# Six projections of two transformer blocks in units of 512 rows by 512 columns, with fox values behind the fox queries and keys

## The chip, the cores and the metric

The kernel runs on 1 core of a Trainium2 chip. The metric is the device time of one execution in microseconds (us). Three runs of the kernel before took 976.42, 976.95 and 977.11 us, median 976.95.

## The reference

The kernel computes two blocks in sequence on 256 tokens of width 1024, in float32. What matters here are the projections of the normed tokens and what uses them:

```python
h = _rmsnorm(x, norm_mix_g[l])
z = h @ w_in[l]                      # 1024 -> hq hf hi hg | fq fk fv ff | mq | gates
(hq, hf, hi, hg, fq, fk, fv, ff, mq, gate_logits) = jnp.split(z, pts, axis=-1)
y_a = _hgrn2_mixer(hq, hf, hi, hg, lower_bounds[l], hgrn_norm_g[l])      # 4 heads of 128
y_b = _fox_mixer(fq, fk, fv, ff, ...)     # 8 heads of 64, softmax of q.k + decay, causal
mem_kv = _rmsnorm(mem, norm_mem_g[l]) @ mem_kv_w[l]                      # mk, mv
y_c = _memory_mixer(mq, mem_kv, ...)      # 4 heads of 128, attention into 256 memory rows
merged = sum(gates[:, :, i] * (y_i @ w_br_i))
x = x + merged @ w_out;  x = x + conv_glu_ffn(rmsnorm(x))
# second block
x = x + 0.5 * swiglu(rmsnorm(x))
qa, ka, va, qb, kb, vb = split(rmsnorm(x) @ w_in_2)   # each 512 wide
x = x + concat(diff_attention(qa, ka, va), dilated_attention(qb, kb, vb)) @ w_out_2
x = rmsnorm(x + 0.5 * swiglu(rmsnorm(x)))
```

Each of hg, hi, fv, mq, mv and vb is one product of a 256 x 1024 matrix with a 1024 x 512 one, with tokens as rows of the result. fq and fk need a root mean square over each head before they meet.

## The kernel before, in words

**Split products.** Every product is done to float32 accuracy by splitting both operands into a high and a low part. `three` issues three matmuls for each 128 rows of the contraction: high by high, high by low, low by high.

**Units.** The weights are a list of units of 128 x 2048 elements (1 MB), made by `weight_plan`. SyncE's queue loads a unit into `raw`, of which there are three; ScalarE writes its high part into `wh` (L975, called by `begin` and `hi_to`), VectorE the low part into `wl` (L1415, `lo_to`). TensorE waits for `w_lo` before it uses a unit, and ScalarE writes unit j when TensorE has ended unit j - 3 (`unit_end`). `begin(key)` on ScalarE and VectorE stands for: prepare the units up to two behind `key`. Since each engine works through its instructions in order, the place of a `begin` is also the place at which everything behind it may wait.

**A projection.** A projection of 512 columns is two units of all 1024 rows by 256 columns. `toks_out` (tokens as rows of the result) takes one bank of the PSUM, and for each half m of the tokens it issues 8 x 3 matmuls of 256 columns, with the transposed normed tokens `hT` as stationary side. ScalarE empties the bank with two instructions (`toks_scaled`, L1009 and L1010), each scaled by the token's norm. `W` (banks 0 and 1) and `WF` (0, 1, 6, 7) hand out banks in turn. `mid` is a function that `toks_out` calls between the two halves; it puts small attention matmuls between the large ones.

**The fox stage** (fox and memory attention of the first block, 141 to 250 us). TensorE issues fq 0, fk 0, fv 0, two transposes for the hgrn branch (`turn(("rd", p))`), fq 1, the transposes of the normed heads (`head_turn`), fk 1 and so on. ScalarE's `head_norm` empties a bank and squares it (L1140), VectorE's `head_sum` adds the squares up (L1720), and GpSimd makes the inverse root (`head_rstd`, L2151 to L2162) and scales the heads (`head_scaled`, L2212). ScalarE also writes the forget sums into the keys for all heads (`fk_made`, two instructions at L1168), VectorE those of the queries (`fox_row`, eight at L1739), and copies the transposed heads out of the PSUM (`fox_out`, L1734). Only then can `scores(0, 0)` run (L656). Behind it come the minimum of the scores (`guards`, L1785), the exponentials (`exps`, L1154), the division (`shares`, L1750), the transposes (`turns`, L670), their `copies` (L1797) and the products with the values (`pair_values`, L703). `step(a, s, t, vs)` issues on TensorE the scores of map s, the values of the maps vs and the transposes of map t.

**The end of the second mixer** (735 to 770 us). vb 0 and vb 1 alternate with the last steps; then come the output projection's units `wo`, which already have 512 rows by 512 columns: `stretch` issues 12 matmuls of 512 columns for one half of the tokens (`weight_wide`), and `half_done` counts the units that end in the middle of a sum.

Of the kernel before, what the change touches and what calls it, by code (L numbers as in the profile page):

```python
# [92 lines left out]

def weight_plan(I):
    w_in, w_in2 = I["w_in"], I["w_in_2"]
    plan = []
    plan += [(("hf", u), cols(w_in, 512 + 256 * u)) for u in range(2)]
    plan += [(("hq", u), cols(w_in, 256 * u)) for u in range(2)]
    plan += [(("hg", u), cols(w_in, 1536 + 256 * u)) for u in range(2)]
    plan += [("ff", cols(w_in, 3584, 8))]  # L100
    plan += [(("hi", u), cols(w_in, 1024 + 256 * u)) for u in range(2)]
    plan += [(("gate", u), cols(w_in, 4104 + 256 * u)) for u in range(12)]
    for u in range(2):
        plan += [((name, u), cols(w_in, a + 256 * u)) for name, a in (("fq", 2048), ("fk", 2560), ("fv", 3072))]
    plan += [(("mq", u), cols(w_in, 3592 + 256 * u)) for u in range(2)]
# [4 lines left out]
    plan += [(("mv", u), cols(I["mem_kv_w"], 512 + 256 * u)) for u in range(2)]  # L110
# [4 lines left out]
    for name, u, a in (("qa", 0, 0), ("ka", 0, 512), ("va", 0, 1024), ("qa", 1, 0), ("ka", 1, 512), ("va", 1, 1024),  # L115
                       ("qb", 0, 1536), ("kb", 0, 2048), ("qb", 1, 1536), ("kb", 1, 2048), ("vb", 0, 2560), ("vb", 1, 2560)):
        plan += [((name, u), cols(w_in2, a + 256 * u))]
    plan += wide_units(4, I["w_out_2"])
# [12 lines left out]
def build(nc, plan, I, out):  # L131
    ctx = ExitStack()
    with ctx:
# [218 lines left out]
        def pe_program(pe):  # L352
# [88 lines left out]

            def turn(key, src, p, n, split=True):
# [90 lines left out]
            for u in range(2):  # L533
                toks_out(("hg", u), WF)
# [9 lines left out]
            toks_out(("hi", 0), WF)  # L544
# [6 lines left out]
            toks_out(("hi", 1), WF)  # L551
# [157 lines left out]
            def mem_values(i):  # L709
                h = i - 8  # L710
                if h % 2 == 0:
                    take(("mo", h // 2), 6 + h // 2, False)
                    turn_no["mo", h // 2] = len(turn_no) + 1
                    pe.wait_ge(*free(("mv", h // 2)))
# [39 lines left out]
            for key in (("fq", 0), ("fk", 0), ("fv", 0)):  # L754
                toks_out(key, W)
# [16 lines left out]
            toks_out(("mq", 0), W, mid=other_fox_heads)  # L772
            step(0, 4, 3)
            toks_out(("mq", 1), W, mid=lambda: step(0, 5, None, [2, 3]))
# [162 lines left out]
            toks_out(("vb", 0), W, mid=lambda: step(1, 12, 10))  # L937
# [4 lines left out]
            toks_out(("vb", 1), W, mid=lambda: step(1, 14, 12, [8, 9]))  # L942
            step(1, 15, 13, [10, 11])
# [7 lines left out]
            step(1, None, 14)  # L951
# [11 lines left out]
        def act_program(act):  # L963
# [47 lines left out]

            def gained_hi(p, g, made):
# [43 lines left out]
            for u in range(2):  # L1056
                begin(("hg", u))
                s = v3(Sg[:, :])[:, :, u * 256:u * 256 + 256]
                if u == 0:
                    act.wait_ge(rstd_made, 1)  # L1060
                toks_scaled(s, ("hg", u), rs0)
                act.wait_ge(*seq.now())
                act.wait_ge(*free(("hg", u)))
                act.activation(v3(P[u][:, :]), s, ACT.Sigmoid).then_inc(g_sig, 1)
# [8 lines left out]
            toks_scaled(v3(Iv[:, :])[:, :, 0:256], ("hi", 0), rs0)  # L1073
# [8 lines left out]
            toks_scaled(v3(Iv[:, :])[:, :, 256:512], ("hi", 1), rs0)  # L1082
# [48 lines left out]

            def head_norm(name, u, src, dst, sq):
                n = HEADS.index((name, u))
# [4 lines left out]
                if n >= 2:  # L1138
                    act.wait_ge(h_sum, n if n >= 6 else n - 1)
                act.activation(v3(sq), d, ACT.Square).then_inc(h_sq, 1)  # L1140
# [21 lines left out]
            begin(("fv", 0))  # L1162
            toks_scaled(v3(Vt[:, :])[:, :, 0:256], ("fv", 0), rs0)

            act.wait_ge(*free("fcum"))
            for j in range(2):
                r = ROW[1 - j]
                act.activation(Kf[j].rearrange("p (k n) -> p k n", k=4)[r], F2[r, :].unsqueeze(1).to_broadcast([64, 4, 256]),  # L1168
                               ACT.Identity, scale=fsel[r, 16:17], bias=fsel[r, 17:18]).then_inc(fk_made, 1)
            for p in range(2):  # L1170
                turn_hi_part(("rd", p), yTh, p, col("hg"))
# [1197 lines left out]
```

## Time and profile before

| | |
|---|---|
| runs of the kernel before | 976.42, 976.95, 977.11 us |
| the profiled execution | 976.5 us, its span 974.7 us |
| TensorE busy | 959.8 us (98%), 6422 matmuls |
| TensorE's weight loads | 858.2 us (88%) |
| VectorE busy | 710.2 us (73%) |
| ScalarE busy | 519.4 us (53%) |
| GpSimd busy | 68.7 us (7%) |
| the chain that ended last | TensorE 94%, VectorE 3%, ScalarE 2% |
| DMA | 174.17 MB, mean 179 GB/s |

Matmuls are pipelined, so one is still shown as running when the next has begun: a single 256-column matmul is shown with 0.28 us but the next begins 0.12 us later. TensorE's pace is read from the distance of the starts.

### The profile page before, as it was taken

The page shows a single profiled execution, that of the slowest core. Times are in us where ns is not written, and L with a number is a line of the kernel's source. Part 1 is how long each engine was busy: PE and PEld are TensorE (multiplying, and loading weights), DVE is VectorE, ACT ScalarE, POOL GpSimd, SP SyncE. Part 2 cuts the span into 40 slices and gives each one's busy share as a digit, 9 for nine tenths or more (in the row PEclk, how much of TensorE's full clock was granted, in tenths as well). Part 3 has the DMA queues.
Part 4 walks back from the last instruction along what each step waited for, and adds up shares of the span by engine and source line. Part 5 has one row for each costly group of instructions (what it writes and reads, how often), then busy time and mean ns, then how long its engine had stood idle before and what let it go on. Part 6 is the DMA issues. An engine that isn't in the chain of part 4 may idle for free.

```text
span 974.7 us, 15574 instructions
## 1 busy us (share of the span) xinstructions
PE 959.8 (98%) x6422; PEld 858.2 (88%) x6422; DVE 710.2 (73%) x1013; ACT 519.4 (53%) x658; POOL 68.7 (7%) x150
## 2 busy tenths in 40 slices
PE   7999999999999999999999999999999999999997
PEld 7999999999988888888888888889999788888886
DVE  5589767886777877787786667567678678576666
ACT  6565757555446656554664444446545554443544
POOL 0010223233210000000000000000002000000000
PEclk9999999999999999999999999999999999999999
DMA  9754444443465564655456555553433546555541
GB/s 345 260 177 151 173 155 149 163 144 127 173 227 173 210 216 173 210 179 186 160 175 214 176 206 180 183 198 134 177 131 130 182 143 216 198 190 178 191 151 44
DMA packets 26534, 174.17 MB, mean 179 GB/s; under 512 B 3552, under 2 KB 3808, under 8 KB 6368
## 3 DMA queue, kind: packets, MB, share of 16 engines
q1 hardware_dynamic: 25744, 170.14, 50.0%
q10 hardware_dynamic: 720, 3.04, 0.8%
q8 instruction: 51, 0.84, 0.3%
q14 instruction: 19, 0.16, 0.0%
HBM read 172.12 MB, written 1.05 MB: 178 GB/s over the span
## 4 chain that ended last, share of the span: by engine, by line
PE 94%; DVE 3%; ACT 2%; issue 0%; DMA 0%; POOL 0%; ACTq 0%; DVEq 0%; POOLq 0%
PE ps L371 50%; PE ps L381 25%; PE ps L382 13%; PE ps L656 2%; DVE wl L1415 1%; PE ps L449 1%; PE ps L670 1%; ACT wh L975 1%; PE ps L703 1%; PE ps L573 1%; DMA GT<-in_gains 0%; PE ps L717 0%; PE ps L684 0%; DVE HG L1645 0%; PE ps L463 0%
## 5 line engine op out<-in xcount | busy, mean ns | idle before, releaser
L1415 DVE TENSOR_TENSOR wl<-raw,wh 128x2048 fp32r<-128x2048 f32 x153 | 348.2, 2277 | 66.5 <-ACT wh L975 65.9
L381 PE MATMUL ps<-hT,wh 128*128 128x512 f32 x1056 | 371.5, 395 | 0.2 <-DVE hT L1444 0.2
L975 ACT ACTIVATE wh<-raw 128x2048 fp32r<-128x2048 f32 x156 | 296.3, 1900 | 76.0 <-PE ps L371 70.8
L382 PE MATMUL ps<-hT,wl 128*128 128x256 f32 x1056 | 295.8, 280 | 0.0
L381 PEld LDWEIGHTS ps<-hT,wh 128*128 128x128 f32 x1056 | 198.0, 188 | 46.8 <-issue 0.6
L382 PEld LDWEIGHTS ps<-hT,wl 128*128 128x128 f32 x1056 | 199.4, 189 | 1.2
L371 PE MATMUL ps<-hT,wh 128*128 128x256 f32 (+1 forms) x912 | 170.6, 289 | 7.0 <-DVE wl L1538 6.6
L371 PEld LDWEIGHTS ps<-hT,wh 128*128 128x128 f32 (+1 forms) x912 | 142.7, 192 | 8.7 <-DVE wl L1538 6.6
L371 PE MATMUL ps<-wh,hT 128*128 128x256 f32 (+1 forms) x704 | 142.3, 296 | 1.3 <-DVE wl L1415 1.3
L371 PE MATMUL ps<-hT,wl 128*128 128x256 f32 (+1 forms) x456 | 129.6, 284 | 0.0
L1261 ACT ACTIVATE Am<-ps 128x512 f32<-128x512 f32 x66 | 39.1, 593 | 151.7 <-PE ps L382 149.0
L371 PE MATMUL ps<-wl,yTh 128*128 128x512 f32 (+1 forms) x298 | 117.7, 395 | 0.0
L371 PEld LDWEIGHTS ps<-wh,hT 128*128 128x128 f32 x704 | 113.4, 191 | 4.6 <-issue 2.0
L371 PE MATMUL ps<-wh,yTl 128*128 128x512 f32 (+1 forms) x298 | 117.2, 393 | 0.0
L371 PE MATMUL ps<-wh,yTh 128*128 128x512 f32 (+1 forms) x298 | 117.0, 393 | 0.0
L371 PE MATMUL ps<-wl,hT 128*128 128x256 f32 (+1 forms) x352 | 102.9, 292 | 0.0
L1500 DVE TENSOR_TENSOR PT<-ps,Am 128x256 f32<-128x256 f32 x132 | 49.8, 419 | 69.5 <-ACT Am L1261 69.3
L371 PEld LDWEIGHTS ps<-hT,wl 128*128 128x128 f32 (+1 forms) x456 | 87.3, 192 | 0.2
L371 PEld LDWEIGHTS ps<-wl,hT 128*128 128x128 f32 x352 | 67.3, 191 | 1.2
L371 PEld LDWEIGHTS ps<-wh,yTh 128*128 128x128 f32 x298 | 55.9, 188 | 13.5
L371 PEld LDWEIGHTS ps<-wh,yTl 128*128 128x128 f32 x298 | 55.9, 188 | 12.9
L371 PEld LDWEIGHTS ps<-wl,yTh 128*128 128x128 f32 x298 | 56.0, 188 | 12.0
(253 smaller groups left out, 819.7 us busy)
## 6 DMA issues: line engine op xcount, KB each, us to landing
raw<-in_units SPq DMA_DIRECT2D x155, 1024.0 KB, 4.8
BIGT<-in_bias ACTq DMA_DIRECT2D x1, 2048.0 KB, 7.5
XT<-in_x_turned SPq DMA_DIRECT2D x4, 256.0 KB, 4.7
raw<-in_units SPq DMA_DIRECT2D x4, 256.0 KB, 5.3
raw<-in_units SPq DMA_DIRECT2D x2, 512.0 KB, 7.6
X<-in_x SPq DMA_DIRECT2D x1, 1024.0 KB, 8.2
Hn<-in_mem SPq DMA_DIRECT2D x1, 1024.0 KB, 11.0
XT<-in_mem_turned SPq DMA_DIRECT2D x1, 1024.0 KB, 12.9
```

What stands on the lines that cost most here:

```text
L371: ins = pe.matmul(o, l(k), r(k), start=first and k == ks[0] and j == 0, stop=last and k == ks[-1] and j == 2)
L381: pe.matmul(o, lh(k), hT_both(k), start=first and k == ks[0], stop=False)
L382: ins = pe.matmul(o[:, 256:512], ll(k), hT_at(k)[0], start=False, stop=last and k == ks[-1])
L449: ins = pe.transpose(t[:, q * 128:q * 128 + 128], src[:, m * n + k * 128:m * n + k * 128 + 128], ident)
L573: ins = pe.matmul(t[x:x + w, q * w + w - z:q * w + w], s[:, x:x + w], s[:, x + a:x + a + z], start=True, stop=True)
L656: ins = pe.matmul(t[:, x:z], l, r, start=True, stop=True)
L670: ins = pe.transpose(t[:, j * 128:j * 128 + 128], src[:, o:o + 128], ident)
L703: ins = pe.matmul(o[64 * j:64 * j + 64, 128 * kb:256], v[:, x:x + 64], turned(a, i + j)[:, c], start=kb == 0, stop=kb == 1)
L975: act.activation(wh[j % NS][:, 0:n], raw[j % NR][:, 0:n], ACT.Copy).then_inc(w_hi, 1)
L1261: act.activation(v3(crossed_out(n)), t, ACT.Copy).then_inc(cross_made, 1)
L1415: dve.tensor_tensor(wl[j % NS][:, 0:n], raw[j % NR][:, 0:n], wh[j % NS][:, 0:n].bitcast(F32), ALU.subtract).then_inc(w_lo, 1)
L1500: dve.tensor_tensor(d[:, m, :], t[:, m, :], v3(crossed_out(n))[:, m, :], ALU.add).then_inc(*emptied((key, key + ("x",))[m]))
```

## The change

Six projections (hg, hi, fv, mq, mv, vb) get units of 512 rows by 512 columns. The first unit holds rows 0 to 511 of all columns, the second the rest. `toks_wide` replaces `toks_out` for them: it takes two banks, one for each half m of the tokens, and a unit issues 2 x 4 x 3 matmuls of 512 columns. The sums of both halves stay open between the two units, so both banks are emptied in or after the second unit; the first unit ends with `half_done`. ScalarE empties a bank of 128 x 512 with one instruction (`wide_scaled`).

```diff
+def wide_rows(name, w, a):
+    return [((name, r), block(w, 512 * r, 512, a, 512)) for r in (0, 1)]
...
+            def toks_wide(name, r, banks, mid=None):
+                i = U[name, r]
+                if r == 0:
+                    bs = [banks.take(), banks.take()]
+                weights(i)
+                for m in range(2):
+                    t = take((name, m), bs[m]) if r == 0 else bank[at[name, m][0]]
+                    ins = three(t[:, :], left(hT_at, m), weight_wide(i, r), EIGHT[4 * r:4 * r + 4], r == 0, r == 1)
+                    if r:
+                        ins.then_inc(ps_full[at[name, m][0]], 1)
+                    if m == 0 and mid:
+                        mid()
...
+            def wide_scaled(dst, name, rs, ms=(0, 1)):
+                for m in ms:
+                    act.wait_ge(*full((name, m)))
+                    act.activation(dst[:, m * 512:m * 512 + 512], bank[at[name, m][0]][:, :], ACT.Copy,
+                                   scale=rs[:, m:m + 1]).then_inc(*emptied((name, m)))
```

The fox stage is written in another order on TensorE:

```diff
-            for key in (("fq", 0), ("fk", 0), ("fv", 0)):
+            for key in (("fq", 0), ("fk", 0), ("fq", 1)):
                 toks_out(key, W)
             pe.wait_ge(ya_made, 2)
             for p in range(2):
                 turn(("rd", p), Sg, p, 512)
-            toks_out(("fq", 1), W)
+            toks_out(("fk", 1), W)
             head_turn("fq", 0, E0)
             head_turn("fk", 0, E1)
-            toks_out(("fk", 1), W, mid=lambda: step(0, 0))
+            toks_wide("fv", 0, W, mid=lambda: step(0, 0))
             step(0, 1)
-            toks_out(("fv", 1), W, mid=lambda: step(0, 2, 0))
+            toks_wide("fv", 1, W, mid=lambda: step(0, 2, 0))
```

and at the end of the second mixer the values of maps 8 to 11 move behind the first output stretch, since they now need vb whole:

```diff
-            toks_out(("vb", 1), W, mid=lambda: step(1, 14, 12, [8, 9]))
-            step(1, 15, 13, [10, 11])
+            toks_wide("vb", 1, W, mid=lambda: step(1, 14, 12))
+            step(1, 15, 13)
...
-            step(1, None, 14)
+            step(1, None, 14, [8, 9, 10, 11])
```

ScalarE and VectorE follow. In both, mq's two squares and the two sums now come together, after mq's second unit. On ScalarE, this is the fox stage before, from the square of fk 0 (L1140 Am) to the high part behind the transposes (HG and Vm at L1168 are the broadcasts of the forget sums; wh is the high part of a weight unit):

```order
L1140 ACTIVATE Am<-HG 128x512 [waits ps_free1,a_seq]
L975 ACTIVATE wh1<-raw1 128x2048 [waits raw_in1,ps_full1]
L1009 ACTIVATE Vt<-ps,sm 128x256 [waits ps_full0]
L1010 ACTIVATE Vt<-ps,sm 128x256
L1168 ACTIVATE HG<-F2,C 64x1024 [waits ps_free2]
L1168 ACTIVATE Vm<-F2,C 64x1024
L982 ACTIVATE yTh<-ps,VT 128x512 [waits ps_full3]
L982 ACTIVATE yTh<-ps,VT 128x512 [waits ps_full4]
L975 ACTIVATE wh2<-raw2 128x2048 [waits raw_in2,ps_full0]
L1009 ACTIVATE HG<-ps,sm 128x256 [waits ps_full1]
```

and now (the lines are 26 to 33 higher):

```order
L1166 ACTIVATE Am<-HG 128x512 [waits ps_free1,a_seq]
L1199 ACTIVATE HG<-F2,C 64x1024 [waits ps_free2]
L1199 ACTIVATE Vm<-F2,C 64x1024
L1001 ACTIVATE wh1<-raw1 128x2048 [waits raw_in1,ps_full1]
L1035 ACTIVATE HG<-ps,sm 128x256 [waits ps_full0]
L1036 ACTIVATE HG<-ps,sm 128x256
L1166 ACTIVATE Ax<-HG 128x512 [waits h_sum,ps_free0,a_seq]
L1008 ACTIVATE yTh<-ps,VT 128x512 [waits ps_full3]
L1008 ACTIVATE yTh<-ps,VT 128x512 [waits ps_full4]
L1001 ACTIVATE wh2<-raw2 128x2048 [waits raw_in2,ps_full0]
L1035 ACTIVATE HG<-ps,sm 128x256 [waits ps_full1]
```

The broadcasts now follow the square of fk 0 directly. They stand ahead of the high part of the stage's fifth unit (fk 1 before, fv 0 now), and the eviction into Vt is gone from here.

On VectorE, the same stage before, from the last of the eight fox rows (L1739) to the first guard (L1436 makes the low parts of rd, L1720 is a head sum, L1734 are the copies of the transposed heads, wl is the low part of a weight unit):

```order
L1739 TENSOR_SCALAR Iv<-F2,C 64x256
L1436 SCALAR_TENSOR_TENSOR yTl<-ps,VT,yTh 128x512 [waits turn_hi] x2
L1734 TENSOR_SCALAR HG<-ps,VT 64x512 [waits ps_full5]
L1734 TENSOR_SCALAR Iv<-ps,VT 64x512
L1734 TENSOR_SCALAR HG<-ps,VT 64x512 [waits ps_full2]
L1734 TENSOR_SCALAR Vm<-ps,VT 64x512
L1415 TENSOR_TENSOR wl2<-raw2,wh2 128x2048 [waits w_hi]
L1785 ISA ps,sm<-ps,C 128x128 [waits ps_full3]
```

and now:

```order
L1776 TENSOR_SCALAR Iv<-F2,C 64x256
L1757 TENSOR_REDUCE sm<-Ax 128x8 [waits h_sq]
L1473 SCALAR_TENSOR_TENSOR yTl<-ps,VT,yTh 128x512 [waits turn_hi] x2
L1452 TENSOR_TENSOR wl2<-raw2,wh2 128x2048 [waits w_hi]
L1757 TENSOR_REDUCE sm<-Am 128x8 [waits h_sq]
L1771 TENSOR_SCALAR HG<-ps,VT 64x512 [waits ps_full5]
L1771 TENSOR_SCALAR Iv<-ps,VT 64x512
L1771 TENSOR_SCALAR HG<-ps,VT 64x512 [waits ps_full2]
L1771 TENSOR_SCALAR Vm<-ps,VT 64x512
L1452 TENSOR_TENSOR wl0<-raw0,wh0 128x2048 [waits w_hi]
L1822 ISA ps,sm<-ps,C 128x128 [waits ps_full3]
```

Two sums and one low part of a weight unit stand between the last fox row and the copies into HG, Iv, HG and Vm; the low part that stood behind the copies is still there.

On TensorE, the end of vb before (L703 is the product with the values, L670 the transposes, L371 with yTh the first output stretch):

```order
L656 MATMUL ps<-HG 128x128 [waits ps_free5]
L656 MATMUL ps<-HG 128x256
L703 MATMUL ps<-Hn,Vm 64x256 [waits ps_free4,ps_free2]
L703 MATMUL ps<-Hn,Vm 64x256
L703 MATMUL ps<-Hn,Vm 64x128 x2
L670 MATMUL ps<-C,P1 128x128 [waits share_made,ps_free2]
L670 MATMUL ps<-C,P1 128x128 x2
L371 MATMUL ps<-wh1,yTh 128x512 [waits ps_free5,w_lo,ps_free2,ps_free1,ps_free0]
```

and now, up to the output stretch:

```order
L682 MATMUL ps<-HG 128x128 [waits ps_free5]
L682 MATMUL ps<-HG 128x256
L696 MATMUL ps<-C,P1 128x128 [waits share_made,ps_free2]
L696 MATMUL ps<-C,P1 128x128 x2
L377 MATMUL ps<-wh1,yTh 128x512 [waits ps_free5,w_lo,ps_free2,ps_free1,ps_free0]
```

The values between the scores and the transposes are gone, and the output stretch waits for the same banks.

## Rows read from the trace of the kernel before

**Rows 1.** The page, part 1: busy us (share of the span) and instructions.
```profile
PE 959.8 (98%) x6422; PEld 858.2 (88%) x6422; DVE 710.2 (73%) x1013; ACT 519.4 (53%) x658; POOL 68.7 (7%) x150
```

**Rows 2.** Timeline of TensorE: start, us, engine, line, op, out<-in, count, idle before.
```profile
33.60 0.36 PE L371 MATMUL ps<-wh,hT 128*128 128x256 f32 x1 [1.32 <-DVE wl L1415]
...
45.18 0.40 PE L371 MATMUL ps<-hT,wh 128*8 128x256 f32 x2
...
275.21 0.40 PE L371 MATMUL ps<-wh,hT 128*128 128x512 f32 x1
...
280.70 0.39 PE L371 MATMUL ps<-wh,yTh 128*128 128x512 f32 x1
```

**Rows 3.** The chain that ended last, at the first gates: start, us, what.
```profile
64.41 2.19 DVE wl L1415
66.74 5.99 PE ps L371 x48
```

**Rows 4.** Timeline of ScalarE in the fox stage.
```profile
153.97 1.90 ACT L975 ACTIVATE wh<-raw 128x2048 fp32r<-128x2048 f32 x1
...
159.13 1.24 ACT L1168 ACTIVATE HG<-F,C 64x1024 f32<-64x1024 f32 x1
...
161.54 1.24 ACT L982 ACTIVATE yTh<-ps,VT 128x512 fp32r<-128x512 f32 x2
```

**Rows 5.** Timeline of VectorE in the fox stage.
```profile
158.22 0.42 DVE L1739 TENSOR_SCALAR HG<-F,C 64x256 f32<-64x256 f32 x1
...
161.34 0.40 DVE L1739 TENSOR_SCALAR Iv<-F,C 64x256 f32<-64x256 f32 x1
162.24 1.41 DVE L1436 SCALAR_TENSOR_TENSOR yTl<-ps,VT,yTh 128x512 fp32r<-128x512 f32 x2 [0.50 <-ACT yTh L982]
165.34 0.74 DVE L1734 TENSOR_SCALAR HG<-ps,VT 64x512 f32<-64x512 f32 x1 [1.69 <-PE ps L449]
...
168.47 2.29 DVE L1415 TENSOR_TENSOR wl<-raw,wh 128x2048 fp32r<-128x2048 f32 x1
...
171.38 0.68 DVE L1720 TENSOR_REDUCE sm<-Ax 128x8 f32<-128x512 f32 x1
```

**Rows 6.** Timeline of GpSimd in the fox stage; of GpSimd and VectorE at 744.
```profile
162.18 2.06 POOL L2212 TENSOR_TENSOR HG<-HG,sm 128x512 f32<-128x512 f32 x2
...
743.92 1.90 POOL L2244 TENSOR_TENSOR Sg<-Sg,sm 128x1024 f32<-128x1024 f32 x1
...
744.03 2.14 DVE L1750 TENSOR_SCALAR P<-P,sm 128x128 f32<-128x128 f32 x2
```

**Rows 7.** The chain that ended last, at the first fox scores.
```profile
168.65 0.89 PE ps L656 x4
```

**Rows 8.** Timeline of VectorE and ScalarE at maps 1 to 3.
```profile
174.18 0.29 DVE L1785 CUSTOM_DVE_ANT_0 ps<-ps,C 128x128 f32<-128x128 f32 x1
...
175.75 1.92 ACT L975 ACTIVATE wh<-raw 128x2048 fp32r<-128x2048 f32 x1
...
180.54 0.30 DVE L1785 CUSTOM_DVE_ANT_0 ps<-ps,C 128x128 f32<-128x128 f32 x1
...
181.80 0.55 DVE L1750 TENSOR_SCALAR P<-P,sm 128x128 f32<-128x128 f32 x2
```

**Rows 9.** Timeline of all engines at the end of vb.
```profile
751.23 0.87 PE L703 MATMUL ps<-Hn,Vm 128*64 128x256 f32 x8
...
755.03 0.55 DVE L1750 TENSOR_SCALAR P<-P,sm 128x128 f32<-128x128 f32 x2
...
755.86 0.47 ACT L1010 ACTIVATE Vm<-ps,sm 128x256 f32<-128x256 f32 x1
...
757.14 0.48 PE L371 MATMUL ps<-wh,yTh 128*128 128x512 f32 x1
...
760.02 0.82 PE L670 MATMUL ps<-C,P 128*128 128x128 f32 x6
```

**Rows 10.** TensorE in a window: us, busy (instructions), granted clock, DMA, GB/s.
```profile
6.60:11.00 4.40, 4.36 (x20) 1.00 1.02 359
```

More of the change, by code:

```diff
@@ L109, in weight_plan @@
     plan += [(("mk", u), cols(I["mem_kv_w"], 256 * u)) for u in range(2)]
-    plan += [(("mv", u), cols(I["mem_kv_w"], 512 + 256 * u)) for u in range(2)]
+    plan += wide_rows("mv", I["mem_kv_w"], 512)
     plan += branches[0][1:] + branches[1] + branches[2]
@@ L936, in pe_program @@
             step(1, 11, 9)
-            toks_out(("vb", 0), W, mid=lambda: step(1, 12, 10))
+            toks_wide("vb", 0, W, mid=lambda: step(1, 12, 10))
             step(1, 13, 11)
@@ L1057, in act_program @@
                 begin(("hg", u))
-                s = v3(Sg[:, :])[:, :, u * 256:u * 256 + 256]
+                s = Sg[:, u * 512:u * 512 + 512]
                 if u == 0:
                     act.wait_ge(rstd_made, 1)
-                toks_scaled(s, ("hg", u), rs0)
-                act.wait_ge(*seq.now())
+                wide_scaled(Sg, "hg", rs0, (u,))
                 act.wait_ge(*free(("hg", u)))
-                act.activation(v3(P[u][:, :]), s, ACT.Sigmoid).then_inc(g_sig, 1)
+                act.activation(P[u][:, :], s, ACT.Sigmoid).then_inc(g_sig, 1)
             begin("ff")
@@ L1129, in act_program, with head_squares @@
                 gate_sigmoid(j)
+            def head_squares(name, u, d, sq):
+                n = HEADS.index((name, u))
+                if n >= 2:
+                    act.wait_ge(h_sum, n if n >= 6 else n - 1)
+                act.activation(v3(sq), d, ACT.Square).then_inc(h_sq, 1)
             def head_norm(name, u, src, dst, sq):
-                n = HEADS.index((name, u))
                 d = v3(dst)[:, :, u * 256:u * 256 + 256]
@@ L1169, in act_program @@
                                ACT.Identity, scale=fsel[r, 16:17], bias=fsel[r, 17:18]).then_inc(fk_made, 1)
+            begin(("fq", 1))
+            head_norm("fq", 1, rs0, E0, sq_a)
             for p in range(2):
                 turn_hi_part(("rd", p), yTh, p, col("hg"))
-            begin(("fq", 1))
-            head_norm("fq", 1, rs0, E0, sq_a)
             begin(("fk", 1))
+            head_norm("fk", 1, rs0, E1, sq_b)
+            begin(("fv", 0))
             exps(0, 0)
-            head_norm("fk", 1, rs0, E1, sq_b)
             exps(0, 1)
             begin(("fv", 1))
+            wide_scaled(Vt, "fv", rs0, (0,))
             exps(0, 2)
-            toks_scaled(v3(Vt[:, :])[:, :, 256:512], ("fv", 1), rs0)
+            wide_scaled(Vt, "fv", rs0, (1,))
             exps(0, 3)
             begin(("mq", 0))
-            act.wait_ge(*full(("ht", "fq", 0)))
-            head_norm("mq", 0, rs0, E0, sq_a)
             exps(0, 4)
             begin(("mq", 1))
+            for u in range(2):
+                act.wait_ge(*full(("ht", "fq", u)))
+            wide_scaled(E0, "mq", rs0, (0,))
             exps(0, 5)
-            act.wait_ge(*full(("ht", "fq", 1)))
-            head_norm("mq", 1, rs0, E0, sq_b)
+            wide_scaled(E0, "mq", rs0, (1,))
+            for m in range(2):
+                act.wait_ge(*free(("mq", m)))
+            for u, sq in enumerate((sq_a, sq_b)):
+                head_squares("mq", u, v3(E0)[:, :, u * 256:u * 256 + 256], sq)
             exps(0, 6)
@@ L1832, in dve_program @@
             shares(0, 1)
-            begin(("fv", 1))
             guards(0, 3)
```

69 lines of the change are left out of this document (36 added, 33 removed).

## The prediction

> **What bounds the kernel.** I read the page first. TensorE is busy 98% of the span [rows 1], so the question is which of its instructions get cheaper and where it will have to wait. The second view is TensorE's timeline, for its pace, since the durations of overlapping matmuls overstate it. From the first narrow matmul of hg to the first of ff, the 96 matmuls of 256 columns take 45.18 - 33.60 = 11.58 us, 0.121 us each. In the output projection, 24 matmuls of 512 columns with hT as the stationary side take 280.70 - 275.21 = 5.49 us, 0.229 us each [rows 2]. So a matmul costs about 13 ns beyond its columns, and half as many matmuls save that. The third view is the chain of waits and the timelines of VectorE and ScalarE, for how far the cover reaches where instructions change places: in the fox stage TensorE and VectorE already meet within 0.2 us.
>
> **Part 1, the wide units.** A projection was two units of 48 narrow matmuls and becomes two units of 24 wide ones: 11.58 - 2 x 5.49 = 0.6 us less each, 3.6 us for six [rows 2]. The bound below this is a pace as with yT as stationary side, about 0.1 us less per unit, so 1.3 us less in all. The weight units keep their number and size; each still costs ScalarE 1.90 us and VectorE 2.29 us [rows 4, 5] in units of 5.5 us, hidden behind matmuls. The evictions are as many columns in half as many instructions, also hidden.
>
> The Trainium skill ("TensorE: Matmul & The Clock Gate", section "Back-to-back issue gap") gives a spacing of N/2.4 + 2.5 ns. By that fixed part the 288 matmuls saved would be worth 0.7 us and not 3.6; rows 2 show about 13 ns, and I go by them.
>
> **Part 2, hg and hi.** TensorE gets through them 1.2 us earlier, but after that the first gates wait for VectorE: the low part of gate unit 1 is made after the scan, ends at 66.60, and TensorE begins at 66.74 [rows 3]. This chain starts at hg's last eviction, about 0.6 us earlier now, and ScalarE leaves hi's first eviction out of it. I move it by 0.7 us, and TensorE gains only this: **-0.7 us** (bounds 0 and -1.2).
>
> **Part 3, the fox stage, which decides.** Three moves act together. ScalarE's two broadcasts into the keys (L1168) now stand ahead of the high part of the stage's fifth unit (now fv's first), where they stood behind it. VectorE's low part of that unit stands ahead of the eight fox rows, as before, so these now wait for the broadcasts too. And ahead of the four copies that the first scores need (fox_out), VectorE now has two head sums (fq 1 and fk 1) and one more low part. Step by step, on the clock of the profile before:
> - ScalarE starts the broadcasts at 153.97, where it started the high part; they take 161.54 - 159.13 = 2.4 us, then the high part 1.90: ready at 158.3 [rows 4].
> - VectorE: low part 2.3, to 160.6. Eight fox rows: 161.34 + 0.40 - 158.22 = 3.5 [rows 5]. They now fall under GpSimd's two products, 2.06 us [rows 6]. At 744.03 a tensor_scalar that reads SBUF took 2.14 us beside a GpSimd product that began at 743.92 [rows 6], and 0.55 otherwise [rows 8]. Fully blocked adds 2.1, not at all 0; I take 1.4, since it is blocked in that row but the eight rows would be somewhat faster without GpSimd's small instructions. To 165.5.
> - Sum of fq 1 0.6, low parts of rd 1.35, low part of a unit 2.25, sum of fk 1 0.6, and four copies 168.47 - 165.34 = 3.1 [rows 5]: to 173.4. Scores begin 0.2 later, at 173.6.
> - TensorE is there at 168.5, since the wide half unit ends as the narrow one did; before, its scores began at 168.65 [rows 7]. **Wait: 5.1 us** (bounds 3.6 and 5.8).
>
> Behind this wait stand the other half of fv's first unit and all that follows on TensorE; nothing later on the path has slack to give it back, as TensorE is the bound everywhere.
>
> A second wait follows at the transposes of head 1. From the start of scores 1 TensorE has about 7.8 us of its own work to them. The other side has the scores (0.7), guard and exponential 1.6 (174.18 to 175.75), the high part 1.90 and low part 2.29 of mq's second unit, which now stand ahead of guard 2, and then guard, copy and share, 1.8 (180.54 to 182.35) [rows 4, 5, 8]: 8.3, with the latencies 8.5. **Wait: 0.7 us** (bounds 0 and 1.3).
>
> mq's two squares and sums now come together after its last matmul. That puts the scaled heads 0.6 us later relative to TensorE, but TensorE has two branch stretches and mk's first unit before it turns them, more than 10 us: no cost. fv and mq save 4 units x 0.3. Sum of the stage: 5.1 + 0.7 - 1.2 = **+4.6 us** (bounds 2.4 and 5.9).
>
> **Part 4, mv.** Each half is used late, and nothing near it waits: **-0.6 us**.
>
> **Part 5, vb.** The values of maps 8 to 11 need vb whole and move behind the first output stretch. VectorE's share of map 13 ends at about 755.5, and it does not come earlier, since its chain runs over VectorE and ScalarE. TensorE, without 2 x 0.8 us of values [rows 9], arrives at 754.9 and waits; turns, then the output stretch from 756.2, when ScalarE has emptied vb's second bank (755.5 plus 0.6; before, 755.86 + 0.47, and the stretch at 757.14), 2.8 us, then 1.6 us of values: 760.6 at the transposes that began at 760.02 [rows 9]. **+0.6 us** in spite of wide units (bounds -0.6 and +0.9).
>
> **Sum.** -0.7 + 4.6 - 0.6 + 0.6 = +3.9 us. The profiled execution took 976.5 us (span 974.7), so 980.4; it is 0.45 below the median of the runs, 976.95, so a median of 980.9. About 0.2%, 2 us, is the least that a measurement of this kernel tells from no change.
>
> **Rivals.**
> - *The clock falls in the wait.* In its first 4.4 us TensorE ran 20 matmuls [rows 10], one per 0.213 us, against 0.120 later: the lower level (1.2 GHz) after 6.6 us of nothing, though the granted clock in the row says 1.00. A wait of 1.3 us at 33.60 [rows 2] did not bring this back. 5.1 us lies between. If it does, 20 x 0.093 = 1.9 us more: 982.8. For it: by far the longest wait in the program. Against it: no wait in this trace shows it. The Trainium skill has it as a rule (same page, "Part 1: The HAM clock gate"): idle time throttles the array again.
> - *The queue is in time, and the change is not slower.* If the fox rows run before the broadcasts' high part is waited for, or ScalarE gets the broadcasts in earlier, both fox waits vanish and only the sums of saved overhead are left: -0.7 - 1.2 - 0.6 + 0.6 = -1.9, so 975.0. The point that decides is the end of the fox copies on VectorE: if it comes before 169.4, when the wait is under 1.2 us and the total under zero. Against it: VectorE is an in-order queue, and the 15 us of work between 158.3 and the copies' end are counted from rows.
> - *The wait is there but shorter.* GpSimd does not block the fox rows and the second wait falls away: 980.9 - 1.4 - 0.7 = 978.8.
> - *The wide matmul is no faster here.* 512 columns at yT's pace: 980.9 + 1.3 = 982.2.
>
> **Chances.** Forecast 0.45; clock 0.17; shorter wait 0.14; no wait 0.14; pace 0.10. The predicted time is the forecast's, 980.9. Its own range is 979.6 to 982. The range takes in the clock's case and the shorter wait's: 977.8 to 983.3. Faster by over 0.2% 0.13 (the case without waits, some of it within), within 0.2% 0.12, slower 0.75.
>
> **What would show it.** In the profile after: TensorE's timeline has an idle stretch of about 5 us before the first fox scores, ended by VectorE's last fox copy; the broadcasts stand right behind fk 0's square on ScalarE; fox rows spaced wider beside GpSimd's products; 24 wide matmuls of a hT unit take 5.5 us; gate unit 1 begins about 0.7 us earlier; the second output projection begins its first stretch earlier and its last transposes later. If the idle before the scores is under 1.2 us, the prediction is wrong in Part 3; if matmuls behind it are spaced as in the first 4 us, the clock rival is right.

## The result and the profile after

| | before | after |
|---|---|---|
| median of four runs each | 976.94 us (976.42 to 977.11) | 984.30 us (983.75 to 984.40) |
| the profiled execution, its span | 976.5, 974.7 us | 984.21, 982.4 us |
| mean granted clock over the span | 0.999 | 0.995 |

The ratio is 1.0077, with a 95% interval of 1.0065 to 1.0089: slower by 7.4 us, where 3.9 were forecast. The direction and the place were right and the size was not.

Part 1 of the page after, to be held against [rows 1]. TensorE has 288 matmuls fewer, and the sum of their durations is not less:

```profile
PE 960.3 (98%) x6134; PEld 844.4 (86%) x6134; DVE 711.1 (72%) x1013; ACT 517.0 (53%) x646; POOL 68.7 (7%) x150
```

The view of TensorE's waits (engine, line, what it waited for: us in total, times, longest) has three larger kinds that the kernel before did not have, those for "issue", for VectorE's P and for GpSimd's HG (two more, for VectorE's Vm and HG, are of 0.2 us each and are left out here):

```profile
PE ps L682 <- issue: 4.9, 1, 4.9
...
PE ps L696 <- DVE P L1787: 1.4, 2, 0.9
PE ps L475 <- POOL HG L2249: 0.3, 1, 0.3
```

"issue" is the name of the largest of the three. It means only that the view found no releaser. VectorE's timeline names it. The last of the four fox copies (L1771) ends at 171.99 + 0.76 = 172.75, and the scores (L682) begin at 172.96. These rows of VectorE after (start, duration, then as in the rows before) answer to [rows 5]:

```profile
157.96 2.29 DVE L1452 TENSOR_TENSOR wl<-raw,wh 128x2048 fp32r<-128x2048 f32 x1 [3.65 <-ACT wh L1001]
160.28 0.42 DVE L1776 TENSOR_SCALAR HG<-F,C 64x256 f32<-64x256 f32 x1
...
161.17 1.02 DVE L1776 TENSOR_SCALAR HG<-F,C 64x256 f32<-64x256 f32 x1
162.23 1.02 DVE L1776 TENSOR_SCALAR Iv<-F,C 64x256 f32<-64x256 f32 x1
...
164.62 0.41 DVE L1776 TENSOR_SCALAR Iv<-F,C 64x256 f32<-64x256 f32 x1
164.95 0.67 DVE L1757 TENSOR_REDUCE sm<-Ax 128x8 f32<-128x512 f32 x1
165.54 1.39 DVE L1473 SCALAR_TENSOR_TENSOR yTl<-ps,VT,yTh 128x512 fp32r<-128x512 f32 x2
166.86 2.27 DVE L1452 TENSOR_TENSOR wl<-raw,wh 128x2048 fp32r<-128x2048 f32 x1
169.06 0.67 DVE L1757 TENSOR_REDUCE sm<-Am 128x8 f32<-128x512 f32 x1
169.66 0.73 DVE L1771 TENSOR_SCALAR HG<-ps,VT 64x512 f32<-64x512 f32 x1
...
171.99 0.76 DVE L1771 TENSOR_SCALAR Vm<-ps,VT 64x512 f32<-64x512 f32 x1
```

It is the queue of the prediction, item by item. VectorE waits 3.65 us for the high part, which stands behind the broadcasts. Then come the low part, eight fox rows, a sum, the low parts of rd, another low part, a sum, and only then the copies. Two of the eight fox rows take 1.02 us instead of 0.42, beside GpSimd's products.

On TensorE, what follows that wait is as important as the wait:

```profile
167.63 0.39 PE L377 MATMUL ps<-wh,hT 128*128 128x512 f32 x1
172.96 1.62 PE L682 MATMUL ps<-HG 128*128 128x128 f32 x4 [4.93 <-issue]
174.02 0.99 PE L377 MATMUL ps<-wh,hT 128*128 128x512 f32 x1
174.80 0.63 PE L377 MATMUL ps<-wl,hT 128*128 128x512 f32 x1
175.23 1.05 PE L377 MATMUL ps<-wh,hT 128*128 128x512 f32 x2
176.08 0.63 PE L377 MATMUL ps<-wl,hT 128*128 128x512 f32 x1
...
178.92 0.81 PE L682 MATMUL ps<-Vm,Iv 128*128 128x128 f32 x4
```

From 174.80 to 176.08 three wide matmuls begin, (176.08 - 174.80) / 3 = 0.427 us each; in the unit of [rows 2] it was 0.229. The windows of the same trace (stretch, length, busy time of each engine, granted clock, DMA share, GB/s) show the clock ahead of the wait, behind it and one stretch later:

```profile
165.00:167.90 2.90, 2.90 (x15) 2.17 (x13) 2.90 (x5) 2.80 (x4) 0.00 (x0) 1.00 0.00 0
174.80:178.00 3.20, 3.20 (x9) 2.52 (x8) 1.07 (x5) 0.91 (x4) 2.88 (x5) 0.50 0.59 159
179.40:182.30 2.90, 2.90 (x14) 2.40 (x13) 1.31 (x7) 1.75 (x5) 0.00 (x0) 1.00 0.00 0
```

0.50 of 2.4 GHz is the lower level, 1.2 GHz. The Trainium skill ("TensorE: Matmul & The Clock Gate", section "Back-to-back issue gap") gives a spacing of N/1.2 ns for that level; by it 512 columns are an estimated 427 ns, and the trace agrees, with 427.

Where the 7.7 us between the two spans came in is read from the starts of the same instruction on TensorE in both timelines (us):

| instruction | before | after | difference | what came in since the row above |
|---|---|---|---|---|
| first level products of the hgrn branch (L573, now L599) | 72.66 | 72.16 | -0.50 | hg and hi |
| fox scores of map 0 | 168.65 | 172.96 | +4.31 | the first wait |
| fox scores of map 1 | 172.24 | 178.92 | +6.68 | the half clock |
| fox scores of map 3 | 179.61 | 186.07 | +6.47 | wide units |
| transposes of map 1 | 180.26 | 187.45 | +7.19 | the second wait |
| last fox scores but one | 197.19 | 204.11 | +6.92 | wide units |
| head turn of mk 0 | 222.64 | 229.96 | +7.32 | a wait for GpSimd |
| head turn of mk 1 | 233.42 | 240.50 | +7.08 | mv |
| scores of map 14 of mixer 2 | 750.49 | 757.41 | +6.92 | |
| transposes of map 14 | 760.02 | 767.64 | +7.62 | vb |

### The profile page after: what moved, and what is told of

It reads as the page before. It is cut to its first block, busy times and chain, and to the rows that moved or that the text cites. A ratio compares the mean times of both kernels' runs of the same rounds, so it can differ in the third digit from the quotient of the medians.

```text
span 982.4 us, 14976 instructions
## 1 busy us (share of the span) xinstructions
PE 960.3 (98%) x6134; PEld 844.4 (86%) x6134; DVE 711.1 (72%) x1013; ACT 517.0 (53%) x646; POOL 68.7 (7%) x150
## 4 chain that ended last, share of the span: by engine, by line
PE 87%; DVE 8%; ACT 3%; issue 1%; POOL 1%; DMA 0%; ACTq 0%; DVEq 0%; POOLq 0%
PE ps L377 44%; PE ps L387 24%; PE ps L388 13%; DVE wl L1452 3%; PE ps L682 2%; ACT wh L1001 1%; PE ps L475 1%; PE ps L696 1%; PE ps L599 1%; PE ps L729 0%; DVE ps L1822 0%; DVE P L1787 0%; DMA GT<-in_gains 0%; PE ps L743 0%; DVE hT L1568 0%
## 5 line engine op out<-in xcount | busy, mean ns | idle before, releaser
L377 PE MATMUL ps<-wh,hT 128*128 128x512 f32 (+1 forms) x512 | 134.7, 346 | 1.4 <-DVE wl L1452 1.4
L377 PEld LDWEIGHTS ps<-wh,hT 128*128 128x128 f32 x512 | 89.4, 192 | 12.7 <-DVE wl L1452 1.9
L377 PE MATMUL ps<-wl,hT 128*128 128x512 f32 (+1 forms) x256 | 86.9, 340 | 0.0
L1187 ACT ACTIVATE P<-ps,sm 128x256 f32<-128x256 f32 (+1 forms) x56 | 23.5, 425 | 62.6 <-DVE sm L1822 47.6
```

Source lines behind the costliest of these rows:

```text
L377: ins = pe.matmul(o, l(k), r(k), start=first and k == ks[0] and j == 0, stop=last and k == ks[-1] and j == 2)
L1187: act.activation(P[i % 2][:, x:z], t[:, x:z], ACT.Exp, bias=mn[:, c], scale=-1.0, accum_out=den[:, c]).then_inc(*(emptied(key) if m else s ...
```

## The experiments

In all, "before" is the kernel before on the same chip, in the same runs. The experiments ran on three chips, with medians of 976.67, 976.54 and 976.83 us for the kernel before, so a difference of some tenths between two experiments is better read from the ratios.

Each execution's mean granted clock is on record too, and it says more than the one profile of a kernel. In the 125 executions, in these experiments, of the kernel before and of `a1`, `a3`, `c1`, `c2`, `d1` and `d2`, which have no long idle stretch in the fox stage, it is never below 0.998. In the profiled execution of `c3`, with some 3 us at half, it is 0.997, and in the four of the change 0.995 or 0.996. So 0.999 is taken here for an execution in which the clock stayed whole in the fox stage, and 0.997 or less for one in which it fell; 0.998 leaves it open (the profiled execution of `a4`, where it fell, has 0.998).

**Undo the fox stage.** In `a1_fox_undone` the plan, TensorE, ScalarE and VectorE have the old code for fq, fk, fv and mq:

```diff
-            for key in (("fq", 0), ("fk", 0), ("fq", 1)):
+            for key in (("fq", 0), ("fk", 0), ("fv", 0)):
...
-            toks_wide("fv", 0, W, mid=lambda: step(0, 0))
+            toks_out(("fk", 1), W, mid=lambda: step(0, 0))
...
-            toks_wide("mq", 1, W, mid=lambda: step(0, 5, None, [2, 3]))
+            toks_out(("mq", 1), W, mid=lambda: step(0, 5, None, [2, 3]))
```

> The changed kernel with the fox stage as before: narrow units of fv and mq and the old order on TensorE, ScalarE and VectorE; hg, hi, mv and vb stay wide. Theory 1 (all of the loss is made in the fox stage: idle 5.1 us before the first fox scores, half the TensorE pace behind it, a second wait): the start of the fox scores stands about 0.5 us before that of the kernel before, mv gives some tenths, vb costs 0.7; total 976.4 to 977.0, no different from the kernel before. Theory 2 (wide units cost a little in each place where two PSUM banks are held through two units, and fox only shows it most): 978 to 980.

Measured: 976.08 us against 976.67 (ratio 0.9994, 0.9985 to 1.0003), so the whole loss is made in the fox stage. Hg and hi gain in it what they gained in the change: its profiled execution is 0.76 us late at 28.80, ahead of every changed unit, and 0.29 late at 72.66.

**One queue, then both.** In `a2_dve_order` only VectorE's order is changed, in `c3_act_order` only ScalarE's, in `a3_both_orders` both, and there guard 2 too, as in `c4_dve_order_2` below:

```diff
 a2, VectorE
             for p in range(2):
                 turn_lo_part(("rd", p), yTh, yTl, p, col("hg"))
+            fox_out("fq", 0, Qf, -0.125)
+            fox_out("fk", 0, Kf, 1.0)
             begin(("fk", 1))
+            guards(0, 0)
             head_sum("fk", 1, sq_b, hss, 64)
-            fox_out("fq", 0, Qf, -0.125)
-            fox_out("fk", 0, Kf, 1.0)
             begin(("fv", 0))
-            guards(0, 0)
 c3, ScalarE
+            begin(("fq", 1))
             act.wait_ge(*free("fcum"))
             ...
-            begin(("fq", 1))
             head_norm("fq", 1, rs0, E0, sq_a)
```

> The changed kernel with one thing moved on VectorE: the four fox copies stand ahead of the low part of fv's second unit and of the sum of fk 1; the broadcasts on ScalarE stay where the change put them. Theory 1 (the copies are late because of what is queued before them): low part to 160.3, eight fox rows to 165.0, sum of fq 1 and low parts of rd to 167.0, copies to 170.1, so scores at 170.2 instead of 172.96 and an idle stretch of 2.3 us. If TensorE's pace behind it stays half for 5 us: 981.5. If a wait of 2.3 us leaves the pace whole: 979.1. Theory 2 (the copies wait for TensorE's head turns, not for the queue): unchanged, 984.3.

Measured: 981.03 us against 976.67 (1.0050, 1.0037 to 1.0063). The first wait is 2.3 us as expected, but the near hit of the total is an accident. In the profiled execution the clock stayed whole (mean 0.999), and the 2.4 us saved by this went into something that I had not counted: the transposes of map 1 now came 2.8 us late by the pace (2.66 idle in the row), for VectorE. The other four executions have a mean clock of 0.997, so in them it fell, and three of them are none the slower (980.88 to 981.03, the profiled one 982.13). That the second wait hides what the clock costs there is an explanation that no experiment tested.

```profile
181.88 0.82 PE L682 MATMUL ps<-Vm,Iv 128*128 128x128 f32 x4
185.36 0.52 PE L696 MATMUL ps<-C,P 128*128 128x128 f32 x3 [2.66 <-DVE P L1787]
```

> The changed kernel with one thing moved on ScalarE: the high part of the fifth unit ahead of the two broadcasts, as before; VectorE's order as the change has it. Theory 1: low part of the unit ends 2.4 us earlier, the fox rows with it, then low part and sum of fk 1 (its square ends at 166.0) to 167.0, copies to 170.1, scores at 170.2: idle 2.3 us instead of 5.1, short enough for the clock as in a2, and the second wait stays at 0.8: 984.3 - 2.8 - 2.4 = 979.1. Theory 2 (the clock falls by the sum of the small waits around the scores as well): 981.5.

Measured: 980.17 us against 976.54 (1.0036, 1.0022 to 1.0049). The wait is 2.05 us, a little shorter than expected, and the clock fell behind it in the profiled execution, contrary to the first theory. It fell in four of the five (0.997, 980.15 to 980.36 us); the fifth, with 0.999, took 979.17, which is the first theory's 979.1.

> The wide units stay all; the order of the kernel before is put back on both engines: on ScalarE the high part of the fifth unit ahead of the two broadcasts, on VectorE the four fox copies ahead of the low part of fv's second unit and the sum of fk 1, and guard 2 ahead of the low part of mq's second unit. Theory 1: fox copies follow the head turns at 165.1 and end at 168.2, scores at 168.4, idle 0.3 us, no half pace, no second wait: 984.3 - 4.8 - 2.4 - 0.7 = 976.4. Theory 2 (the wait comes with the shift of fv behind the keys on TensorE, whatever the queues do): 980 or more.

Measured: 976.42 us against 976.67 (0.9996, 0.9987 to 1.0005). The fox copies follow the head turns at once, and the scores wait no longer than they did before: by the pace they are 0.3 us late, and in the kernel before 0.2.

```profile
164.87 1.04 PE L475 MATMUL ps<-C,HG 128*128 128x128 f32 x8
...
168.82 0.89 PE L682 MATMUL ps<-HG 128*128 128x128 f32 x4
```

So the units may be wide and fv may stand behind the keys on TensorE. The first wait, and the clock behind it, were made by two places in two queues; guard 2, which `a3` moves back too, is tested alone below.

**The second wait.** `c4_dve_order_2` is a2 with one line moved on VectorE, `d4_act_order_2` is c3 with the same:

```diff
-            begin(("fv", 1))
             guards(0, 2)
             copies(0, 0)
             shares(0, 1)
+            begin(("fv", 1))
```

> The kernel a2 with one more thing moved on VectorE: guard 2, copy 0 and share 1 ahead of the low part of mq's second unit, as before. In a2 TensorE waited 2.9 us at 185.36 for the share of map 1. Theory 1 (that low part, and behind it guard 2, made this wait): it goes to 0.3 or less and the total to 981.0 - 2.7 = 978.3. Theory 2 (VectorE is simply 2.9 us behind since the fox rows, and the wait moves on to a later transpose or weight unit): 980.5 or more.

Measured: 979.32 us (1.0028, 1.0017 to 1.0038), 1.7 us less than a2 where 2.7 were expected. In the trace the second wait is gone altogether. Against the kernel before, the first scores are 2.59 us late in a2 and 2.09 here, and the transposes of map 1 are 5.10 late there and 1.79 here. Of that difference of 3.3 us, 0.5 was already there at 28.80, where a2's profiled execution was later, so 2.8 are the wait. The profiled executions took 982.13 and 978.72 us. The medians differ by less, and the clock bears on it: the median execution of c4 is one in which it fell (0.997, 979.32 us), while the three with a whole clock took 978.59 to 978.72, 2.4 us under the median of a2. How much of a2's spread, 980.88 to 983.32, is the clock stays open.

> The kernel c3 (only the broadcasts on ScalarE put back) with guard 2, copy 0 and share 1 ahead of the low part of mq's second unit. The second wait of 0.8 us goes; the idle stretch before the scores stays at about 2.05 us. In the profile of c3 seven matmuls behind that stretch ran at half pace, in those of a2 and c4 none did behind 2.3 us. Theory 1 (the clock fell by the place of the idle stretch, as in c3): again seven or so slow matmuls, 980.2 - 0.8 = 979.4. Theory 2 (the fall belonged to that one execution): none, 978.0.

Measured: 978.59 us (1.0020, 1.0011 to 1.0029), between the two expectations, because both came true. In the profile the idle stretch is again 2.05 us, no matmul behind it is slow and the mean clock is 0.999; the six executions with 0.999 took 977.96 to 978.59 us, near the second theory's 978.0. Two have 0.997 and took 979.26 and 979.46, near the first theory's 979.4; the other three have 0.998 and took 978.92 to 979.59.

**The clock.** 21 wide matmuls are added to the changed kernel. In `a4_pe_filled` they stand behind the waits for the fox copies, in `c1_filled_before` ahead of every wait; `d5_half_filled` has 10 there.

```diff
 c1
+                    if i == 0:
+                        fl, fr = left(hT_at, 0)[0], weight_wide(U["fv", 0], 0)[0]
+                        for f in range(21):
+                            pe.matmul(t[:, :], fl(f % 4), fr(f % 4), start=True, stop=True)
                     if i % 4 == 0:
                         pe.wait_ge(*free(("ht", "fq", i // 4)))
```

> The changed kernel with 21 added matmuls of 512 columns (4.8 us at full pace) at the place of the wait before the first fox scores, into the bank that the scores then overwrite; they only keep TensorE busy. Theory 1 (the half pace behind the wait is the clock, which falls because TensorE did nothing): the same start of the scores, at 173.0, but full pace behind it, 984.3 - 2.4 = 981.9. Theory 2 (the half pace belongs to those matmuls or to transfers of that moment): 984.3 or a little more.

Measured: 988.69 us (1.0125, 1.0111 to 1.0138), neither of the two. The place was my mistake: the wait for the copies comes earlier in the same function, so the added matmuls did not fill the wait but followed it. It still tells something. Now they took the half pace, seven of them at some 0.427 us, and the scores and the half unit of fv behind them ran at full pace. So the slowness belongs to what comes first behind the wait, and not to the fox scores or to that half unit. Nor does it belong to transfers of that moment: the DMA share in this slow window is 0.07, where it was 0.59 in that of the change.

```profile
173.90:176.70 2.80, 2.80 (x7) 2.22 (x8) 2.13 (x1) 0.00 (x0) 2.56 (x3) 0.50 0.07 23
```

> As the kernel a4, with the 21 added matmuls now ahead of every wait of the first fox scores, so that they fill the idle stretch of 5.1 us itself (4.8 us at full pace). Theory 1 (the clock falls in the idle stretch): scores still at 173.0 on the clock of the profile after, full pace behind them: 984.3 - 2.4 = 981.9. Theory 2 (a half pace that follows the wait for another reason, such as the low parts and products of that moment): 984.3.

Measured: 981.62 us against 976.54 (1.0053, 1.0041 to 1.0066), 2.7 less than the change (2.3 by the ratios), as the first theory had it, and the mean clock is 0.998 or 0.999 in all five. The added work fills the wait, the scores begin no earlier, and behind them the clock is whole:

```profile
168.48 4.92 PE L666 MATMUL ps<-wh,hT 128*128 128x512 f32 x21
173.46 0.89 PE L686 MATMUL ps<-HG 128*128 128x128 f32 x4
174.01 0.58 PE L377 MATMUL ps<-wh,hT 128*128 128x512 f32 x1
174.42 0.39 PE L377 MATMUL ps<-wl,hT 128*128 128x512 f32 x1
```

Doing more work than the changed kernel made it faster. This shows that the fall of the clock comes from TensorE's idle time, and that it costs 2.3 to 2.7 us here.

> As c1, but with 10 added matmuls instead of 21 ahead of the waits of the first fox scores, so that 5.1 - 2.3 = 2.8 us of the idle stretch are left behind them. If 2.8 us leave the clock whole: 981.6, as c1. If it falls as behind 5.1 us: 984.0.

Measured: 982.29 us (1.0060, 1.0047 to 1.0073). In the profile the stretch that is left idle is 2.7 us and the clock is whole behind it. Not every execution was like the profiled one: three have a mean clock of 0.998 or 0.999 and took 981.68 to 982.29, and in two it fell (0.997; 982.75 and 983.78).

**vb, hg and hi, mk.** `c2_best` is a3 with vb narrow, `d2_start_undone` is c2 with hg and hi narrow too, `d1_best_mk` is c2 with one line moved on VectorE:

```diff
 c2
-            toks_wide("vb", 1, W, mid=lambda: step(1, 14, 12))
-            step(1, 15, 13)
+            toks_out(("vb", 1), W, mid=lambda: step(1, 14, 12, [8, 9]))
+            step(1, 15, 13, [10, 11])
 d1
+            head_sum("mk", 0, sq_a, mss, 128)
             head_out("mq", 0, G, col("mq"), -(128.0 ** -0.5))
             head_out("mq", 1, G, col("mq"), -(128.0 ** -0.5))
-            head_sum("mk", 0, sq_a, mss, 128)
```

> Both orders put back as in a3 and the last value projection (vb) narrow as before, with values 8 to 11 again inside its two units. Theory 1 (vb costs 0.6 to 0.7 us because TensorE arrives earlier at the share of map 13, waits 1.1 us for it and then still has the values of maps 8 to 11 to do): 976.4 - 0.65 = 975.8. Theory 2 (that wait is passed on to the next stage anyway): 976.4.

Measured: 975.72 us against 976.54 (0.9989, 0.9980 to 0.9998), 0.7 less than a3 and 0.6 less by the ratios, as expected; the two intervals overlap, so times alone do not settle it.

> The kernel c2 with hg and hi narrow as before, so fv, mq and mv alone are wide. Theory 1 (hg and hi gain 0.5 us at the first gates, since VectorE's chain begins that much earlier, and nothing later gives it back): 975.7 + 0.5 = 976.2. Theory 2 (later waits for VectorE and GpSimd swallow it): 975.7 to 975.9.

Measured: 976.23 us against 976.83 (0.9994, 0.9985 to 1.0003), 0.5 more than c2, as expected; a step this small lies within what the intervals leave open.

> The kernel c2 with the sum of mk 0 on VectorE ahead of the two copies of the mq heads. In c2, a3 and the changed kernel TensorE waits 0.4 us before the head turns of mk 0 for GpSimd's product, whose chain starts at that sum. Theory 1 (the chain starts 1.3 us earlier and the wait goes): 975.7 - 0.4 = 975.3. Theory 2 (GpSimd's small instructions then meet the low part on VectorE sooner, are blocked there for its 2.3 us as before, and the product ends at the same time): 975.7.

Measured: **975.10 us against 976.83 (0.9983, 0.9975 to 0.9992)**, the fastest of all kernels here. It is 0.6 us less than c2 (0.9 by the ratios), a step that the intervals leave open as well, but the traces show what was expected to change. In c2 the head turn of mk 0 waits for GpSimd, in d1 it follows at once (first the row of c2, then that of d1):

```profile
221.59 0.66 PE L474 MATMUL ps<-C,HG 128*128 128x128 f32 x4 [0.34 <-POOL HG L2248]
```

```profile
221.76 0.60 PE L474 MATMUL ps<-C,HG 128*128 128x128 f32 x4
```

One of GpSimd's small instructions takes over 2 us beside VectorE's low part in either kernel, but with d1's earlier sum the chain begins earlier and its product does too, although d1's profiled execution was 0.7 us later than c2's at 28.80. These are the rows of c2, then those of d1:

```profile
214.57 2.17 POOL L2187 TENSOR_SCALAR sm<-sm 128x4 f32<-128x4 f32 x1 [7.81 <-DVE sm L1756]
...
220.49 1.04 POOL L2248 TENSOR_TENSOR HG<-HG,sm 128x512 f32<-128x512 f32 x1
```

```profile
215.16 2.34 POOL L2196 TENSOR_SCALAR sm<-sm 128x4 f32<-128x4 f32 x1
...
220.12 1.05 POOL L2248 TENSOR_TENSOR HG<-HG,sm 128x512 f32<-128x512 f32 x1
```

## Why the prediction was right about the place and wrong about the size

**The step that failed is the clock.** The prediction had it as a rival, "the clock falls in the wait", with a chance of 0.17 and a price of 1.9 us; the sum took it at nothing. It was real: 0.50 in the rows behind the wait, and 2.7 us less when the wait was filled (c1). Its argument against was "no wait in this trace shows it", but the only longer waits that the trace had were of 6.6 us, with half pace behind it, and of 1.3 us. The new wait of 5.1 us lay nearer to the first. And the end of the same trace does show a fall: TensorE's last matmul ends at 968.56, the granted clock is still 1.00 up to 973.50, and then it is half, 5 us after TensorE went idle. From the windows of the kernel before:

```profile
971.00:973.50 2.50, 0.00 (x0) 0.00 (x0) 0.49 (x1) 0.46 (x1) 0.00 (x0) 1.00 0.46 175
973.60:974.70 1.10, 0.00 (x0) 0.00 (x0) 0.00 (x0) 0.00 (x0) 0.00 (x0) 0.50 0.13 43
```

With these rows the rival had the better case. The price was too low as well. Scores of map 0 to scores of map 1 took 178.92 - 172.96 = 5.96 us; in a3 they take 172.31 - 168.82 = 3.49. That is 2.5 us: 5.2 us at half pace, where the first stretch of the program has 4.4 [rows 10].

**Fox, first wait (5.1 us): right.** The last matmul ahead of it starts at 167.63 and the scores at 172.96, which is 5.1 us more than the pace. The rows blocked by GpSimd cost 2 x 0.6 = 1.2 us instead of 1.4 (the 2.14 us of [rows 6], which the prediction gives to one instruction, are those of two). The wait was charged whole, though the scores before began at 168.65 and not at 168.5, which is 0.15 us too much. Each of the two orders alone takes away 2.8 to 3.1 us of the wait, together they take all (a2, c3, a3). So "these now wait for the broadcasts too" and "two head sums and one more low part ahead of the copies" were both causes, of about the same size.

**Second wait (0.7 us): right.** The table has 7.19 - 6.47 = 0.7. It is the low part of mq's second unit ahead of guard 2 that makes it (c4, d4).

**hg and hi (-0.7 us): -0.5.** The limit was named rightly; it is what VectorE's chain gains. The unbroken wide units of hg (48 matmuls in 44.53 - 33.48 = 11.05 us, against 11.58 in [rows 2]) save 0.5, near the 0.6 of the sum (at 2.4 GHz the two paces of [rows 2] are 14 and 15 ns above their columns and not 13, which changes nothing, since the 0.6 is taken from starts):

```profile
33.48 0.50 PE L377 MATMUL ps<-wh,hT 128*128 128x512 f32 x1 [1.23 <-DVE wl L1452]
...
44.53 0.40 PE L377 MATMUL ps<-hT,wh 128*8 128x256 f32 x2
```

**fv and mq (-1.2 us): -0.6.** In a3, where no long wait hides it, the start at 72.66 is 0.17 late and that at 197.19 is 0.46 early, against the kernel before. The term took the saving from an unbroken unit. In the fox stage every unit is broken in halves by scores and transposes. Half a unit took 175.76 - 172.71 = 3.05 us narrow and takes 175.74 - 172.78 = 2.96 wide, so 0.1 and not 0.15. The first matmul of a half does not explain this: behind scores the next start comes 0.18 us later than the pace in the narrow form (0.30 us, from 172.71 in the kernel before) and 0.19 in the wide one (0.42 us, from 169.36 in a3). What does stays open.

**mv (-0.6 us): -0.3.** It gains 0.3 in the change (0.2 between the two head turns and 0.1 ahead of the first) and 0.4 in a1, where no wait is near it; its units are broken in halves too. The wait of the table at the head turn of mk 0 is not mv's doing, for a1 has mv wide and has no such wait. It comes from the fox stage, from the step "mq's two squares and sums now come together ... no cost".

**mq's sums (nothing): +0.5.** Both sums now stand where one stood, and VectorE works without a gap from there to the sum of mk 0, which starts GpSimd's chain. So VectorE is 6.92 us late ahead of the second sum and 7.51 behind it and at the sum of mk 0 (222.19, before 214.68), while TensorE is 6.84 us late when it is ready for the head turn of mk 0. GpSimd's product for mk 0 ended at 221.30 + 1.04 = 222.34 before, 0.3 us ahead of the turn; now it ends at 229.91, and TensorE is ready at 229.24 + 0.23 = 229.47. Without the 0.6 us of the second sum the product would have been in time; no run moves this sum alone. The rows are VectorE's two sums and TensorE's turn in the profile after, the product of the kernel before, and the turn in a1:

```profile
206.69 0.68 DVE L1757 TENSOR_REDUCE sm<-Ax 128x4 f32<-128x512 f32 x1
207.28 0.68 DVE L1757 TENSOR_REDUCE sm<-Am 128x4 f32<-128x512 f32 x1
```

```profile
229.96 0.66 PE L475 MATMUL ps<-C,HG 128*128 128x128 f32 x4 [0.34 <-POOL HG L2249]
```

```profile
221.30 1.04 POOL L2212 TENSOR_TENSOR HG<-HG,sm 128x512 f32<-128x512 f32 x1
```

```profile
222.82 0.60 PE L475 MATMUL ps<-C,HG 128*128 128x128 f32 x4
```

**vb (+0.6 us): right, step by step.** TensorE waits at the transposes of map 13 for the share of that map, then goes into the output stretch, and the values come late. By the offset of 6.98 that the trace has at 745.77, the stretch at 763.22 stands for 756.2, and the transposes of map 14 at 767.64 for 760.7; 756.2 and 760.6 were forecast. These rows answer to [rows 9]:

```profile
762.80 0.52 PE L696 MATMUL ps<-C,P 128*128 128x128 f32 x3 [0.85 <-DVE P L1787]
763.22 0.47 PE L377 MATMUL ps<-wh,yTh 128*128 128x512 f32 x1
...
766.19 1.52 PE L729 MATMUL ps<-Hn,Vm 128*64 128x256 f32 x16
767.64 0.55 PE L696 MATMUL ps<-C,P 128*128 128x128 f32 x3
```

**The sum.** Against the forecast of +3.9: the clock +2.5, fv and mq +0.6, the wait at mk 0 +0.5, mv +0.3, hg and hi +0.2, the 0.15 charged too much -0.15, the others about 0. That makes 7.85, and the spans differ by 7.7. With the clock alone at its measured size the forecast would have been 983.4; the rest, about 1 us, is the smaller terms. That vb, the second wait and most of the first came out within 0.1 to 0.2 us is more than the working could promise: their bounds were 1.3 to 2.2 us wide.

## What to carry to other kernels

In this kernel, where TensorE is busy all the time, the change in its instructions was worth less than the order of the two queues that feed it: the same wide units gave 984.3 us in one order of the queues and 976.4 in another. Before an operation is moved ahead in a queue, list what every other engine's queue has behind it, up to the next instruction that the busy engine waits for; the second sum of mq stood more than 20 us ahead of the wait at mk 0. And a wait that a change adds is priced with what follows it: if it may bring TensorE to half its clock, the stretch behind it counts too. One profile is one execution: where the clock is in play, look at the mean clock of every execution.

## What the runs showed of the hardware that was not expected

The clock does not follow the length of the idle stretch alone. Behind 5.1 us it fell in all four executions of the change and in the profiled one of a4. Behind shorter stretches it fell in some executions of a kernel and not in others, by their mean clocks:

| kernel | idle ahead of the scores | fell (0.997) | whole (0.999) | open (0.998) |
|---|---|---|---|---|
| `c3` | 2.05 us | 4 | 1 | 0 |
| `d4` | 2.05 us | 2 | 6 | 3 |
| `a2` | 2.3 us | 4 | 1 | 0 |
| `c4` | 2.3 us | 2 | 3 | 2 |
| `d5` | 2.7 us | 2 | 2 | 1 |

In the profiled executions of the last four it stayed whole, in that of a2 also behind the second wait of 2.8 us. These are the rows of c3, with the clock near half in a window of 2.7 us although the idle stretch was as short as any here:

```profile
170.02 0.89 PE L682 MATMUL ps<-HG 128*128 128x128 f32 x4 [1.89 <-issue]
...
170.98 0.39 PE L377 MATMUL ps<-wl,hT 128*128 128x512 f32 x1
171.21 0.85 PE L377 MATMUL ps<-wh,hT 128*128 128x512 f32 x2
...
172.29 1.05 PE L377 MATMUL ps<-wh,hT 128*128 128x512 f32 x2
173.15 0.63 PE L377 MATMUL ps<-wl,hT 128*128 128x512 f32 x1
```

```profile
172.30:175.00 2.70, 2.70 (x8) 2.11 (x7) 0.65 (x4) 0.91 (x4) 2.47 (x4) 0.53 0.59 173
```

The matmuls right behind the stretch still ran at full pace there (170.98 to 171.21) and slowed down about 1.5 us after the scores had begun. What decides between two executions with the same idle stretch stays open.

The first large matmul behind small ones holds the next one off for longer than the pace, in either form: behind scores 0.30 us with 256 columns (172.71 in the kernel before) and 0.42 with 512 (169.36 in a3), and 0.30 with 512 behind transposes (763.22 to 763.52 in the change), where the paces are 0.12 and 0.23. A unit that is broken in halves by small matmuls gained 2 x 0.09 us from being wide, and an unbroken one (11.58 - 11.05) / 2 = 0.27.
